# SSD chunks: the scaling by the reciprocal deviation is done by ScalarE instead of VectorE

## The chip, the cores and the metric

One core of a Trainium2 chip runs the whole program, a two-block sequence model on 1024 tokens of width 1024 in float32. The metric is the device time of one execution in microseconds (us). In three runs the kernel before took 3720.2, 3724.92 and 3739.85 us, median 3724.92.

Names of engines: PE is TensorE (PEld its weight loads), DVE is VectorE, ACT is ScalarE, POOL is GpSimd, SP is SyncE, which here only starts transfers.

## The reference, cut to what matters

The program computes a first block (short convolutions, a gated linear recurrence, a feed-forward part), then a second block with two mixers, the SSD mixer and an mLSTM, a projection and a routed mixture of experts. The change lies in the SSD mixer alone, in its last step, a norm over each of two groups of 512 channels:

```python
def group_rmsnorm(y, w, groups):
    b, l, c = y.shape
    yg = y.reshape(b, l, groups, c // groups)
    yg = yg * lax.rsqrt(jnp.mean(yg * yg, axis=-1, keepdims=True) + EPS)
    return yg.reshape(b, l, c) * w.astype(jnp.float32)

# inside ssd_mixer, for each chunk: y from inside the chunk, y from the carried state, the new state
cb = jnp.einsum('blgn,bsgn->bgls', c_c, b_c)
y = jnp.einsum('bgls,bgrls,bsgrp->blgrp', cb, lmat, x_c)
y = y + jnp.einsum('blgn,bgrpn,bgrl->blgrp', c_c, state, jnp.exp(a_cs))
...
y = y + d_skip.astype(f32)[:, None] * xs
y = y.reshape(bsz, seq, SSD_WIDTH) * jax.nn.silu(z.astype(f32))
return group_rmsnorm(y, norm_w, SSD_GROUPS).astype(z.dtype)
```

## The kernel before, in words

The function `ssd_chunks` (lines 1498 to 1862) runs the SSD mixer over NC = 8 chunks of 128 tokens. Tokens of a chunk lie on the 128 partitions, the 1024 channels along the free dimension: 16 heads of 64, in G = 2 groups of 8 heads. Each engine has its own written-out order of work, and semaphores tie the engines together. Chunk k's front part is done one chunk early, so each loop step k holds the rest of chunk k and the front of chunk k+1.

What each engine does in step k, in its order:

- **DVE** (lines 1724 to 1770): y of the carried state (L1728, reads PSUM), plus y inside the chunk (L1731, reads PSUM), plus the skip term (L1737), times silu(z) (L1739), the state's update (L1743, reads PSUM). Then for chunk k+1: `inputs` (L1686 xdt and L1689 xdec), `c_by_b` (L1693) and `matrices(k + 1, 0)` (L1699: the decay matrices of the first 8 heads times C by B, 128x1024). Then the reciprocal of chunk k's two deviations (L1751) and the scaling of y by them, two instructions of 128x512 (L1755). Then `matrices(k + 1, 1)` (L1699 again, the other 8 heads), the addition of the former chunk's output product to the residual (`add`, L1713, twice), the gain while the turned y is read from PSUM (L1767, twice), and the low half of the split into two parts for the float32 product (L1770). In step 0 `add` is replaced by the low halves of the second eight weight tiles (`w_low`, L1705).
- **ACT** (lines 1658 to 1676): copies of x and B out of PSUM for chunk k+1 (L1631, L1635), `decay(k + 1, 0)` (L1640, 8 exponentials of 128x128), the squares of y with their sums (L1665), the deviation (L1668, a square root), `decay(k + 1, 1)` (L1640, 8 more), in step 0 also the high halves of the second eight weight tiles (`w_high`, L1646), and at the end the high half of y (L1676). Square root and exponential use different tables, so each step has two table loads.
- **POOL** (lines 1612 to 1620): the state times its decay (L1616), the skip term of chunk k+1 (`skip`, L1605), the causal mask of chunk k+2 (`causal`, L1599: the broadcast cumulated decays plus the mask, 128x2048).
- **PE** (lines 1836 to 1862): y of the carried state (L1841), y inside the chunk (L1847, first and second group of heads each wait for their `matrices`), the new state (L1854), the turns of chunk k+1's x and B (L1794, L1799), C by B (L1806), the output product of chunk k-1 (`out_product`, 48 matmuls, L343 to L345), and last the turns of chunk k's normed y (`result`, L1827).
- **SP** (lines 1551 to 1575): the loads of chunk k+2, which wait for the state product of chunk k (xbc, then the broadcast of the cumulated decays L1559, then z), and at the start the 16 weight tiles of the output product through four buffers, each waiting for the `w_low` three tiles back (L1572).

PSUM's psA has two halves used in turn; `take` lets PE write a half only after its reader is through.

Of the kernel before, what the change touches and what calls it, by code (L numbers as in the profile page):

```python
# [16 lines left out]
ACT = mybir.ActivationFunctionType  # L17
ALU = mybir.AluOpType
# [6 lines left out]
def wait(eng, sem, value):  # L25

    if isinstance(value, int) and value <= 0:
        return
    eng.wait_ge(sem, value)  # L29
# [70 lines left out]
def f32(ap):  # L100
    return ap.bitcast(F32)
# [1396 lines left out]
def ssd_chunks(nc, A, x_tm, hl, scr):  # L1498
# [6 lines left out]
    NC, H, G, W = scr.T, SSD_HEADS, SSD_GROUPS, 1024  # L1505
    HG, HD, XT = H // G, W // H, W // P
    GW, HALF, NS = W // G, 512, 4
    with ExitStack() as ctx:
        c = Core(nc, ctx)
# [7 lines left out]
        x_r, xdt, xdec, xd = (c.sb(f"sd_{n}", [P, W]) for n in ("x", "xdt", "xdec", "xd"))  # L1517
        b_r, cbm = c.sb("sd_b", [P, G, P]), c.sb("sd_cb", [P, G, P])
        lt = c.sb("sd_l", [P, 2, H, P])
        state = c.sb("sd_state", [P, W])  # L1520
        y, sq = c.sb("sd_y", [P, W]), c.sb("sd_sq", [P, W])
        ssq, std, rstd = c.sb("sd_ssq", [P, G]), c.sb("sd_std", [P, G]), c.sb("sd_rstd", [P, G])
# [8 lines left out]
        s_w, s_whi, s_wlo = c.sems("w2_w_loaded", NS), c.sem("w2_w_high"), c.sem("w2_w_low")  # L1531
        (p_sums, p_A, p_cb, p_in, p_inter, p_state, p_w2) = (
            c.sem(f"sd_pe_{n}") for n in ("sums", "psA_written", "cb", "intra", "inter", "state", "out"))
        (a_e, a_A, a_l, a_sq, a_std, a_yh) = (c.sem(f"sd_act_{n}") for n in ("exps", "psA_read", "decay", "squares", "std", "high"))
        (d_xdt, d_xdec, d_cb, d_m, d_y1, d_yb, d_y, d_st, d_ch, d_rs, d_n, d_yt, d_yl, d_add) = (
            c.sem(f"sd_dve_{n}") for n in ("xdt", "xdec", "cb", "m", "y1", "psB_read", "y", "state", "chain", "rstd", "normed",
                                           "yt", "low", "added"))
        (g_x, g_l, g_st) = (c.sem(f"sd_pool_{n}") for n in ("x", "causal", "state"))
        block = ctx.enter_context(nc.Block(no_gpsimd_drain=True))
# [5 lines left out]
        def front_use(k, j):  # L1545
            return j if k == 0 else 5 * k - 2 + j

        def result_use(k, j):
            return 5 * k + (6 if k + 1 < NC else 3) + j
# [72 lines left out]
        @block.scalar  # L1622
        def _(act):
            def front(k):
                if k:
                    act.wait_ge(d_xdt, k)
                    act.wait_ge(g_x, k)
                for j in range(2):
                    n = front_use(k, j)
                    act.wait_ge(p_A, n + 1)  # L1630
                    nc.scalar.activation(x_r[:, j * 512:(j + 1) * 512], psA[:, n % 2], ACT.Copy).then_inc(a_A, 1)  # L1631
                n = front_use(k, 2)
                act.wait_ge(p_A, n + 1)
                wait(act, p_state, k)
                nc.scalar.activation(b_r[:].rearrange("p g n -> p (g n)"), psA[:, n % 2, 0:G * P], ACT.Copy).then_inc(a_A, 1)  # L1635

            def decay(k, g):
                act.wait_ge(g_l, k + 1)
                for h in range(g * HG, (g + 1) * HG):
                    last = nc.scalar.activation(lt[:, k % 2, h], lt[:, k % 2, h], ACT.Exp, bias=ncum[:, k, h:h + 1])  # L1640
                last.then_inc(a_l, 1)

            def w_high(n):
                h, k = divmod(n, XT)
                act.wait_ge(s_w[n % NS], 16 * (n // NS + 1))
                nc.scalar.activation(hl[:, 0, k, h * HALF:(h + 1) * HALF], stage[:, n % NS], ACT.Copy).then_inc(s_whi, 1)  # L1646

            act.wait_ge(s_c1, 6)
            act.wait_ge(p_sums, 1)
            nc.scalar.activation(ncum[:], sums[:, 0], ACT.Copy, scale=-1.0).then_inc(a_e, 1)  # L1650
            nc.scalar.activation(e3[:], sums, ACT.Exp).then_inc(a_e, 1)
            front(0)
            act.wait_ge(a_e, 2)
            decay(0, 0)
            decay(0, 1)
            for n in range(XT):
                w_high(n)
            for k in range(NC):
                if k + 1 < NC:
                    front(k + 1)  # L1660
                    decay(k + 1, 0)
                act.wait_ge(d_y, k + 1)
                for g in range(G):
                    cut = slice(g * GW, (g + 1) * GW)
                    nc.scalar.activation(sq[:, cut], y[:, cut], ACT.Square, accum_out=ssq[:, g:g + 1]).then_inc(a_sq, 1)  # L1665
                act.wait_ge(a_sq, G * (k + 1))
                wait(act, d_rs, k)
                nc.scalar.activation(std[:], ssq[:], ACT.Sqrt, scale=1.0 / GW, bias=eps[:]).then_inc(a_std, 1)  # L1668
                if k + 1 < NC:
                    decay(k + 1, 1)  # L1670
                if k == 0:
                    for n in range(XT, NW):
                        w_high(n)
                act.wait_ge(d_yt, 2 * k + 2)
                wait(act, p_w2, 2 * k)
                nc.scalar.activation(yh[:, 0], yt[:], ACT.Copy).then_inc(a_yh, 1)  # L1676

        @block.vector
        def _(dve):
            v, ch = nc.vector, Chain(dve, d_ch)  # L1680
# [10 lines left out]
            def c_by_b(k):  # L1691
                dve.wait_ge(p_cb, k + 1)
                v.tensor_copy(cbm[:], cbt).then_inc(d_cb, 1)  # L1693
                dve.wait_ge(d_cb, k + 1)
# [29 lines left out]
            for k in range(NC):  # L1724
                if k:
                    dve.wait_ge(p_inter, k)
                    dve.wait_ge(p_A, result_use(k - 1, 1) + 1)
                    v.tensor_tensor(heads(y[:]), both(psC), per_head(e3[:, 0, k]), ALU.mult).then_inc(d_y1, 1)  # L1728
                    dve.wait_ge(d_y1, k)
                    dve.wait_ge(p_in, k + 1)  # L1730
                    v.tensor_tensor(heads(y[:]), heads(y[:]), both(psB), ALU.add).then_inc(d_yb, 1)  # L1731
                else:
                    dve.wait_ge(p_in, 1)
                    v.tensor_copy(heads(y[:]), both(psB)).then_inc(d_yb, 1)
                dve.wait_ge(d_yb, k + 1)
                dve.wait_ge(g_x, k + 1)
                ch.link(v.tensor_tensor(y[:], y[:], xd[:], ALU.add))  # L1737
                dve.wait_ge(s_z[k % 2], 16 * (k // 2 + 1))
                v.tensor_tensor(y[:], y[:], z[:, k % 2], ALU.mult).then_inc(d_y, 1)  # L1739
                dve.wait_ge(p_state, k + 1)  # L1740
                if k:
                    dve.wait_ge(g_st, k)
                    v.tensor_tensor(state[:], state[:], psC[:].rearrange("p a n -> p (a n)"), ALU.add).then_inc(d_st, 1)  # L1743
                else:
                    v.tensor_copy(state[:], psC[:].rearrange("p a n -> p (a n)")).then_inc(d_st, 1)
                if k + 1 < NC:
                    inputs(k + 1)
                    c_by_b(k + 1)
                    matrices(k + 1, 0)
                dve.wait_ge(a_std, k + 1)  # L1750
                v.reciprocal(rstd[:], std[:]).then_inc(d_rs, 1)  # L1751
                dve.wait_ge(d_rs, k + 1)
                for g in range(G):
                    cut = slice(g * GW, (g + 1) * GW)
                    v.tensor_scalar(y[:, cut], y[:, cut], rstd[:, g:g + 1], None, ALU.mult).then_inc(d_n, 1)  # L1755
                if k + 1 < NC:
                    matrices(k + 1, 1)
                if k == 0:
                    for n in range(XT, NW):
                        w_low(n)  # L1760
                else:
                    add(k - 1)
                wait(dve, a_yh, k)
                for j in range(2):
                    n = result_use(k, j)
                    dve.wait_ge(p_A, n + 1)
                    v.tensor_tensor(yt[:, 4 * j:4 * j + 4], quad(n), norm[:, 4 * j:4 * j + 4].unsqueeze(2).to_broadcast([P, 4, P]),  # L1767
                                    ALU.mult).then_inc(d_yt, 1)
                dve.wait_ge(a_yh, k + 1)
                v.tensor_tensor(yh[:, 1], yt[:], f32(yh[:, 0]), ALU.subtract).then_inc(d_yl, 1)  # L1770
# [3 lines left out]
        def _(pe):  # L1774
# [8 lines left out]
            def take(n):  # L1783
                if n >= 2:
                    pe.wait_ge(*readers[n - 2])
# [33 lines left out]
                    last.then_inc(p_w2, 1)  # L1819

            def result(k):
                pe.wait_ge(d_n, G * (k + 1))
                for j in range(2):
                    n = result_use(k, j)
                    take(n)
                    for t in range(4):
                        last = nc.tensor.transpose(quad(n)[:, t], y[:, (4 * j + t) * P:(4 * j + t + 1) * P], ident[:])  # L1827
                    last.then_inc(p_A, 1)
# [1134 lines left out]
```

## Time and profile before

| what | value |
|---|---|
| three runs | 3720.2, 3724.92, 3739.85 us |
| the profiled execution, its own time | 3727.0 us |
| its span, first to last instruction | 3725.2 us |
| mean granted TensorE clock | 0.937 of full speed |
| the SSD chunks within the span | about 2407 to 2640 us |

The profile comes from one profiled execution. Its span is 1.8 us shorter than that execution's own time; what lies around the span is the launch and the end. In a row of the timeline the first number is the start in us from the span's start, the second the length in us, then engine, line, operation, output and inputs, shape, count (x2: two merged in one row). A bracket at the end gives the idle time of the engine before the row and the instruction that ended it. In a row of a line's summary three numbers stand for the shortest, the median and the longest in ns. In a row of stretches the columns are: the stretch in us, its length, busy time of PE, PEld, DVE, ACT and POOL with counts in brackets, the granted TensorE clock, the share of DMA and GB/s.

### The profile page before, as it was taken

What the parts mean: (1) busy time and instruction counts of PE and PEld (TensorE: products, weight loads), DVE (VectorE), ACT (ScalarE), POOL (GpSimd) and SP (SyncE); (2) the same over time, 40 slices, a digit from 0 to 9 for tenths busy, and PEclk for the clock granted to TensorE, in tenths of its full rate; (3) what the DMA queues carried; (4) which work ended last, traced back from release to release, by engine and by line L of the source; (5) the groups of instructions that cost most, each with busy time, mean ns of one, the idle gap of its engine ahead of it and who ended that gap; (6) DMA issues with size and microseconds to landing.
All of it is one profiled execution on the core that took longest, in us unless ns stands there. A gap on an engine that the chain in (4) does not pass through costs nothing. (4 is left out here: it accounts for less than half of the span.)

```text
span 3725.2 us, 39593 instructions
## 1 busy us (share of the span) xinstructions
PE 3361.8 (90%) x15130; PEld 2747.4 (74%) x15130; DVE 1930.8 (52%) x2158; ACT 1374.0 (37%) x1931; POOL 263.9 (7%) x312
## 2 busy tenths in 40 slices
PE   6999999898899999998799999869897859999994
PEld 4888888686788888887687788647787747777773
DVE  3344443433344455445413655188333468888885
ACT  4332332212321111111521323244255328788883
POOL 0000000000000000000010000133000110000002
PEclk9999999998999999999899999979766979999997
DMA  3222222433011111110331233642120239999996
GB/s 98 63 71 83 80 66 70 147 113 118 24 56 51 51 51 43 41 51 10 135 90 64 84 98 96 205 171 77 63 90 29 81 118 378 382 392 393 390 393 236
DMA packets 330352, 489.19 MB, mean 131 GB/s; under 512 B 58736, under 2 KB 230256, under 8 KB 328192
## 3 DMA queue, kind: packets, MB, share of 16 engines
q1 hardware_dynamic: 299776, 380.11, 29.8%
q0 software_dynamic: 25856, 90.78, 6.4%
q10 hardware_dynamic: 4608, 16.78, 1.1%
q8 instruction: 73, 1.20, 0.1%
q14 instruction: 39, 0.32, 0.0%
HBM read 406.28 MB, written 81.33 MB: 131 GB/s over the span
## 5 line engine op out<-in xcount | busy, mean ns | idle before, releaser
L947 DVE TENSOR_TENSOR x_rows<-x_rows,ff_psd 128x512 f32<-128x512 f32 x352 | 239.5, 688 | 334.5 <-PE ff_psd L345 334.5
L343 PE MATMUL m_ps<-h_hl,m_w_hl 128*128 128x512 f32 x896 | 356.7, 398 | 11.6 <-DVE m_w_hl L530 11.6
L345 PE MATMUL m_ps<-h_hl,m_w_hl 128*128 128x512 f32 x896 | 350.3, 391 | 0.0
L344 PE MATMUL m_ps<-h_hl,m_w_hl 128*128 128x512 f32 x896 | 350.2, 391 | 0.0
L2471 DVE TENSOR_TENSOR h_hl<-ex_stage,h_hl 128x1024 fp32r<-128x1024 f32 x256 | 306.1, 1222 | 45.2 <-ACT h_hl L2467 43.9
L2467 ACT ACTIVATE h_hl<-ex_stage 128x1024 fp32r<-128x1024 f32 x256 | 269.7, 1059 | 87.4 <-DMA ex_stage<-in_exp_w_up_dram 50.1
L343 PE MATMUL pj_turned<-h_hl,pc_w_hl 128*128 128x512 f32 x576 | 226.0, 392 | 6.1 <-DVE pc_w_hl L1310 6.1
L345 PE MATMUL pj_turned<-h_hl,pc_w_hl 128*128 128x512 f32 x576 | 225.0, 391 | 0.0
L344 PE MATMUL pj_turned<-h_hl,pc_w_hl 128*128 128x512 f32 x576 | 225.0, 391 | 0.0
L343 PEld LDWEIGHTS m_ps<-h_hl,m_w_hl 128*128 128x128 f32 x896 | 169.1, 189 | 50.5 <-DVE m_w_hl L530 12.0
L927 ACT ACTIVATE ff_act_hl<-ff_act 128x1024 fp32r<-128x1024 f32 x22 | 23.3, 1060 | 485.3 <-DVE ff_act L965 485.3
L344 PEld LDWEIGHTS m_ps<-h_hl,m_w_hl 128*128 128x128 f32 x896 | 169.0, 189 | 38.5 <-issue 3.8
L345 PEld LDWEIGHTS m_ps<-h_hl,m_w_hl 128*128 128x128 f32 x896 | 168.9, 188 | 35.2
L2471 DVE TENSOR_TENSOR ex_w_hl<-ex_stage,ex_w_hl 128x1024 fp32r<-128x1024 f32 x128 | 153.8, 1222 | 36.8 <-ACT ex_w_hl L2467 36.3
L530 DVE TENSOR_TENSOR m_w_hl<-m_stage,m_w_hl 128x1024 fp32r<-128x1024 f32 x56 | 68.5, 1223 | 193.9 <-ACT m_w_hl L458 193.9
L343 PE MATMUL ff_psg<-h_hl,ff_wg 128*128 128x512 f32 x352 | 139.9, 397 | 21.6 <-PE ff_psd L345 10.9
L2467 ACT ACTIVATE ex_w_hl<-ex_stage 128x1024 fp32r<-128x1024 f32 x128 | 132.8, 1057 | 45.5 <-DMA ex_stage<-in_exp_w_gate_dram 36.0
L343 PE MATMUL ff_psd<-ff_wd,ff_act_hl 128*128 128x512 f32 x352 | 138.2, 393 | 4.3 <-DVE ff_act_hl L967 4.3
L345 PE MATMUL ff_psg<-h_hl,ff_wg 128*128 128x512 f32 x352 | 138.0, 392 | 0.0
L344 PE MATMUL ff_psd<-ff_wd,ff_act_hl 128*128 128x512 f32 x352 | 138.0, 392 | 0.0
L344 PE MATMUL ff_psg<-h_hl,ff_wg 128*128 128x512 f32 x352 | 138.0, 392 | 0.0
L345 PE MATMUL ff_psd<-ff_wd,ff_act_hl 128*128 128x512 f32 x352 | 137.8, 391 | 0.0
(508 smaller groups left out, 7701.3 us busy)
## 6 DMA issues: line engine op xcount, KB each, us to landing
ex_stage<-in_exp_w_gate_dram SPq DMA_DIRECT2D x128, 512.0 KB, 5.5
ex_stage<-in_exp_w_up_dram SPq DMA_DIRECT2D x128, 512.0 KB, 7.6
ex_stage<-in_exp_w_down_dram SPq DMA_DIRECT2D x128, 512.0 KB, 6.3
m_stage<-in_w_in_dram SPq DMA_DIRECT2D x56, 512.0 KB, 4.2
pc_stage<-in_w_in_dram SPq DMA_DIRECT2D x36, 512.0 KB, 3.7
scratch_ys<-ex_ys ACTq DMA_DIRECT2D x32, 512.0 KB, 7.3
ff_stage<-in_w_ffn_gate_dram SPq DMA_DIRECT2D x22, 512.0 KB, 4.7
ff_stage<-in_w_ffn_up_dram SPq DMA_DIRECT2D x22, 512.0 KB, 6.0
```

The costliest lines, as they stand in the source:

```text
L343: nc.tensor.matmul(out, w_hl[0], x_hl[0], start=first, stop=False)
L344: nc.tensor.matmul(out, w_hl[0], x_hl[1], start=False, stop=False)
L345: return nc.tensor.matmul(out, w_hl[1], x_hl[0], start=False, stop=last)
L530: v.tensor_tensor(w_hl[s][:, 1], stage[:, s], f32(w_hl[s][:, 0]), ALU.subtract).then_inc(s_lo, 1)
L927: nc.scalar.activation(a_hl[b][:, 0], act_f[:], ACT.Copy).then_inc(s_ah, 1)
L947: v.tensor_tensor(dst, dst, ps_d[g % NB][:], ALU.add).then_inc(s_add, 1)
L2467: nc.scalar.activation(w_hl[u][:, 0], stage[:, s], ACT.Copy).then_inc(s_hi, 1)
L2471: nc.vector.tensor_tensor(w_hl[u][:, 1], stage[:, slot(e, u)], f32(w_hl[u][:, 0]), ALU.subtract).then_inc(s_lo, 1)
```

## The change

The two scalings leave the DVE's order, where they stood behind the reciprocal, and enter ACT's order behind the square root and ahead of `decay(k + 1, 1)`. ACT now waits for the reciprocal before them. DVE's reciprocal waits for the former chunk's scalings, since they read what it overwrites. PE's turns of y wait for ACT instead of DVE.

```diff
@@ ACT, step k
                 act.wait_ge(a_sq, G * (k + 1))
                 wait(act, d_rs, k)
                 nc.scalar.activation(std[:], ssq[:], ACT.Sqrt, scale=1.0 / GW, bias=eps[:]).then_inc(a_std, 1)
+                act.wait_ge(d_rs, k + 1)
+                for g in range(G):
+                    cut = slice(g * GW, (g + 1) * GW)
+                    nc.scalar.activation(y[:, cut], y[:, cut], ACT.Copy, scale=rstd[:, g:g + 1]).then_inc(a_n, 1)
                 if k + 1 < NC:
                     decay(k + 1, 1)
@@ DVE, step k
                 dve.wait_ge(a_std, k + 1)
+                wait(dve, a_n, G * k)
                 v.reciprocal(rstd[:], std[:]).then_inc(d_rs, 1)
-                dve.wait_ge(d_rs, k + 1)
-                for g in range(G):
-                    cut = slice(g * GW, (g + 1) * GW)
-                    v.tensor_scalar(y[:, cut], y[:, cut], rstd[:, g:g + 1], None, ALU.mult).then_inc(d_n, 1)
                 if k + 1 < NC:
                     matrices(k + 1, 1)
@@ PE, result(k)
-                pe.wait_ge(d_n, G * (k + 1))
+                pe.wait_ge(a_n, G * (k + 1))
```

## Rows read from the trace of the kernel before

**Rows 1.** The page, part 1: busy time of each engine over the span

```profile
PE 3361.8 (90%) x15130; PEld 2747.4 (74%) x15130; DVE 1930.8 (52%) x2158; ACT 1374.0 (37%) x1931; POOL 263.9 (7%) x312
```

**Rows 2.** Stretches: chunk 2 and chunk 5 of the SSD stage

```profile
2496.80:2518.90 22.10, 21.03 (x112) 16.48 (x112) 20.77 (x20) 11.41 (x27) 9.26 (x3) 1.00 0.27 108
...
2563.10:2587.00 23.90, 22.83 (x113) 17.12 (x112) 22.15 (x20) 11.41 (x27) 9.79 (x3) 0.93 0.26 100
```

**Rows 3.** Summary of line 1755, all chunks

```profile
L1755 DVE TENSOR_SCALAR sd_y<-sd_y,sd_rstd x16: 473/484/4667, 2456.6 to 2619.4; 128x512 f32<-128x512 f32 x16
```

**Rows 4.** Timeline of DVE in chunk 2

```profile
2506.53 1.23 DVE L1699 TENSOR_TENSOR sd_l<-sd_l,sd_cb 128x1024 f32<-128x1024 f32 x1
...
2507.67 0.16 DVE L1751 RECIPROCAL sd_rstd<-sd_std 128x2 f32<-128x2 f32 x1
...
2507.87 5.06 DVE L1755 TENSOR_SCALAR sd_y<-sd_y,sd_rstd 128x512 f32<-128x512 f32 x2
...
2512.85 1.21 DVE L1699 TENSOR_TENSOR sd_l<-sd_l,sd_cb 128x1024 f32<-128x1024 f32 x1
...
2517.58 1.39 DVE L1770 TENSOR_TENSOR sd_y_hl<-sd_yt,sd_y_hl 128x1024 fp32r<-128x1024 f32 x1 [1.12 <-ACT sd_y_hl L1676]
```

**Rows 5.** Timeline of POOL in chunk 2

```profile
2506.79 5.46 POOL L1599 TENSOR_TENSOR sd_l<-sd_cum_l,sd_neg 128x2048 f32<-128x2048 f32 x1 [2.97 <-DMA sd_cum_l<-scratch_cum]
...
2515.99 1.90 POOL L1616 TENSOR_TENSOR sd_state<-sd_state,sd_e 128x1024 f32<-128x1024 f32 x1 [3.74 <-PE sd_psC L1841]
```

**Rows 6.** Timeline of ACT in chunk 2

```profile
2506.98 0.29 ACT L1668 ACTIVATE sd_std<-sd_ssq,sd_eps 128x2 f32<-128x2 f32 x1
...
2507.30 1.28 ACT L1640 ACT_TABLE_LOAD   x1
...
2508.59 2.45 ACT L1640 ACTIVATE sd_l<-sd_l,sd_neg_cum 128x128 f32<-128x128 f32 x8
```

**Rows 7.** Summaries of ACT lines: exponentials, copies, a copy with a scale per partition

```profile
L1640 ACT ACTIVATE sd_l<-sd_l,sd_neg_cum x128: 384/388/404, 2419.3 to 2602.5; 128x128 f32<-128x128 f32 x128
...
L1646 ACT ACTIVATE h_hl<-w_stage x16: 615/631/635, 2434.6 to 2466.4; 128x512 fp32r<-128x512 f32 x16
...
L1676 ACT ACTIVATE sd_y_hl<-sd_yt x8: 1056/1057/1057, 2469.0 to 2628.9; 128x1024 fp32r<-128x1024 f32 x8
...
L232 ACT ACTIVATE n_xn<-x_rows,n_rstd x32: 1131/1146/1154, 10.8 to 2998.9; 128x1024 f32<-128x1024 f32 x32
```

**Rows 8.** Timeline of DVE in chunk 0

```profile
2456.38 0.16 DVE L1751 RECIPROCAL sd_rstd<-sd_std 128x2 f32<-128x2 f32 x1
...
2457.37 1.22 DVE L1699 TENSOR_TENSOR sd_l<-sd_l,sd_cb 128x1024 f32<-128x1024 f32 x1
```

**Rows 9.** Timeline of DVE in chunk 1

```profile
2484.35 5.58 DVE L1699 TENSOR_TENSOR sd_l<-sd_l,sd_cb 128x1024 f32<-128x1024 f32 x1
...
2489.86 0.15 DVE L1751 RECIPROCAL sd_rstd<-sd_std 128x2 f32<-128x2 f32 x1
...
2490.85 1.22 DVE L1699 TENSOR_TENSOR sd_l<-sd_l,sd_cb 128x1024 f32<-128x1024 f32 x1
```

**Rows 10.** Timeline of POOL in chunk 1

```profile
2484.23 4.63 POOL L1599 TENSOR_TENSOR sd_l<-sd_cum_l,sd_neg 128x2048 f32<-128x2048 f32 x1 [2.58 <-DMA sd_cum_l<-scratch_cum]
...
2493.88 1.90 POOL L1616 TENSOR_TENSOR sd_state<-sd_state,sd_e 128x1024 f32<-128x1024 f32 x1 [5.03 <-PE sd_psC L1841]
```

**Rows 11.** Timeline of PE: the state product of chunks 1 and 2

```profile
2472.48 2.93 PE L1854 MATMUL sd_psC<-sd_xdec,sd_b 128*128 128x512 f32 x3 [6.42 <-DVE sd_y L1728]
...
2498.05 1.98 PE L1854 MATMUL sd_psC<-sd_xdec,sd_b 128*128 128x512 f32 x4 [0.73 <-DVE sd_y L1728]
```

**Rows 12.** Timeline of DVE in chunk 6

```profile
2599.16 0.17 DVE L1751 RECIPROCAL sd_rstd<-sd_std 128x2 f32<-128x2 f32 x1
...
2602.93 1.23 DVE L1699 TENSOR_TENSOR sd_l<-sd_l,sd_cb 128x1024 f32<-128x1024 f32 x1 [2.68 <-ACT sd_l L1640]
...
2608.23 2.61 DVE L1770 TENSOR_TENSOR sd_y_hl<-sd_yt,sd_y_hl 128x1024 fp32r<-128x1024 f32 x1 [1.12 <-ACT sd_y_hl L1676]
```

More of the change, by code:

```diff
@@ L1533, in ssd_chunks @@
             c.sem(f"sd_pe_{n}") for n in ("sums", "psA_written", "cb", "intra", "inter", "state", "out"))
-        (a_e, a_A, a_l, a_sq, a_std, a_yh) = (c.sem(f"sd_act_{n}") for n in ("exps", "psA_read", "decay", "squares", "std", "high"))
-        (d_xdt, d_xdec, d_cb, d_m, d_y1, d_yb, d_y, d_st, d_ch, d_rs, d_n, d_yt, d_yl, d_add) = (
-            c.sem(f"sd_dve_{n}") for n in ("xdt", "xdec", "cb", "m", "y1", "psB_read", "y", "state", "chain", "rstd", "normed",
+        (a_e, a_A, a_l, a_sq, a_std, a_yh, a_n) = (c.sem(f"sd_act_{n}") for n in ("exps", "psA_read", "decay", "squares", "std", "high", "normed"))
+        (d_xdt, d_xdec, d_cb, d_m, d_y1, d_yb, d_y, d_st, d_ch, d_rs, d_yt, d_yl, d_add) = (
+            c.sem(f"sd_dve_{n}") for n in ("xdt", "xdec", "cb", "m", "y1", "psB_read", "y", "state", "chain", "rstd",
                                            "yt", "low", "added"))
```

## The prediction

> **What bounds the kernel now.** The page's busy shares [rows 1] are means over the whole program and say little: the change touches only the SSD stage, 233 us of the span. I read the stretches of that stage chunk by chunk: DVE is busy 20.77 of 22.10 us in chunk 2, PE 21.03 of 22.10 at full granted clock [rows 2]. Chunks 3 and 4 look the same. So DVE and PE are both nearly full here, while ACT works half the time.
>
> The summary of line 1755 shows what the change is aimed at: a scaling takes 0.48 us in the median but 4.67 us at worst [rows 3]. The timelines show the cause. In chunk 2 the pair starts at 2507.87 while POOL's mask sum runs from 2506.79 to 2512.25, and takes 5.06 us instead of 0.88 [rows 4, 5]. Chunks 2 to 5, four of eight, have it; the other four pairs take 0.88. In chunk 1 the same mask sum starts 0.12 us ahead of `matrices(2, 0)`, and that instruction is the one stretched, to 5.58 us against 1.22 [rows 9, 10]. So it is not the scaling that is special: the DVE instruction that comes while POOL's runs is held to its end. In the rows the L1699 of 1.21 us, the L1770 and the scaling all behave so, the reciprocal of two columns does not [rows 4].
>
> What decides the change stands beside this on ACT. After the deviation (ends 2507.27) come the table load, 1.28 us, and eight exponentials, 2.45 us, which end at 2511.04 [rows 6]. DVE's next instruction, the second L1699, needs them. DVE asks for them only at 2512.85 [rows 4]: DVE's stall covers the exponentials.
>
> **The change part by part.** The yardstick is the stretch from the end of the reciprocal to the start of the second L1699.
>
> Removed from DVE: the pair, 5.06 us in four chunks and 0.88 in four [rows 3, 4].
>
> Added to ACT, behind the reciprocal: two copies of 128x512 with a scale per partition. The plain copy of that size takes 0.63 us. A scale per partition costs the copy of 1024 columns 1.146 - 1.057 = 0.09 us [rows 7]. So 0.72 each; neighbours overlap, since eight exponentials of 0.388 (sum 3.10) take 2.45, or 0.09 at each of seven joints [rows 6, 7]. Two come to 2 x 0.72 - 0.09 = 1.35 us. Bounds: 1.17 without the scale's extra, 1.44 without overlap.
>
> Moved on ACT: table load and exponentials now stand behind that. The new stretch from the reciprocal's end is 0.03 (a semaphore, as from 2507.27 to 2507.30 [rows 6]) + 1.35 + 0.03 + 1.28 + 0.01 + 2.45 + 0.03 = 5.18 us. Bounds 5.0 and 5.3. No table load is added: between square root and exponential one is there already, and line 1676's copies follow either function without one.
>
> The Trainium skill (ScalarE: Activation LUTs, What ACT_TABLE_LOAD costs) adds about 1.38 us of drain to a switch of tables. Here the exponentials start 0.01 us after the load, so the trace does not agree; with the page's figure the stretch would be 6.6 us and the whole sum some 8 us higher.
>
> Chunks 2 to 5: the reciprocal ends at 2507.83 in chunk 2, so L1699 starts at 2513.0 instead of 2512.85: +0.16 us [rows 4]. The mask sum is over by then, so it isn't stretched. Even 0.16 is hidden: L1770 is held to 1.39 us by POOL's state scaling (ends 2517.89), which PE's order releases, not DVE's [rows 4, 5]. It ends at 2518.97 either way. Four times zero: **the 4.2 us stall that goes is replaced by a wait for ACT of the same length.**
>
> Chunk 0: no stall was there. The reciprocal ends at 2456.54; L1699 moves from 2457.37 [rows 8] to 2461.72, **+4.35 us**. Behind it are the low halves of eight weight tiles, and SP's last four weight loads and chunk 2's loads wait for these, so SP's queue moves along and nothing absorbs it. On ACT the high halves queue behind the exponentials and shift by as much.
>
> Chunk 1: the reciprocal ends at 2490.01, after L1699's stall. The second L1699 moves from 2490.85 to 2495.19. PE's turns, after the last scaling, come at 2491.4 instead of 2490.99, and with them POOL's state scaling goes from 2493.88 to about 2494.3, ending 2496.2 [rows 9, 10]. L1699 now falls into it and is held until 1.08 us after its end (as L1770 in chunk 2): ends 2497.3 instead of 2492.07, **+5.2 us**.
>
> Chunk 2, PE: its state product waits for DVE's L1728. That idle time was 0.73 us and is then 4 to 5 us. In chunk 1, after 6.42 us of idling, three matmuls took 0.98 us apiece against 0.50 [rows 11]: the lower of the two clock levels. What this costs a chunk is the difference of chunk 5 (granted 0.93) and chunk 2 (1.00): 23.9 - 22.1 = **1.8 us** [rows 2]. Bounds 0 and 1.8; I take it whole, since the idle time is nearer to the 6.42 than to the 0.73.
>
> Chunk 6: the pair took 0.88 and DVE waited 2.68 us for ACT already; L1699 moves from 2602.93 to 2599.33 + 5.18 = 2604.5, +1.6, of which the adds' wait for PE takes some. The rest goes into L1770's stretch, 2.61 against 1.22, a slack of 1.39 [rows 12]: zero, bound 0.5. Chunk 7 has no second L1699, and its turns on PE wait for the output product beyond both dates: zero. POOL's queue issues no transfer in these chunks.
>
> Sum: 4.35 + 5.2 + 1.8 = 11.35 us. The profiled execution took 3727.0 us, so 3738.4 against its own time. It lies 2.1 us above the median of 3724.92, so against the median 3736.
>
> **The rivals.** *The freed stall counts (faster).* If the exponentials were not late, DVE would win 4 x 5.06 + 4 x 0.88 = 23.8 us: 3701. For it: DVE is 94% busy. Against it: the 5.18 us of ACT's new chain, and POOL's hold on L1770, which would eat the gain even then. Half of it would be 3713. Chance 0.04.
>
> *Chunk 1 slips out (a little slower).* The mask sum starts only 0.12 us ahead of L1699 there [rows 9, 10]. If it starts behind, L1699 runs through in 1.2, the reciprocal comes 4.4 us earlier, and chunk 1 costs nothing, as chunk 2 does. Left is chunk 0: +4.4, 3729. Chance 0.2.
>
> *The stall lands ahead of the reciprocal in more chunks (slower).* In chunk 2 the first L1699 starts 0.26 us before the mask sum, whose transfer decides when [rows 4, 5]. Before, the order didn't matter: the chunk lost one stall either way. After the change the order matters: a stretched L1699 delays the reciprocal, and the 5.18 us come on top. Each chunk that turns pays what chunk 1 pays, 5.2 us. One gives 3741; all four of chunks 2 to 5 give 11.35 + 20.8 = 32, 3757. It is slower by over 0.5% (18.6 us) from the second chunk on. Chance of exactly one 0.2, of more 0.09.
>
> The Trainium skill (SBUF — State Buffer, SBUF: two separate sides) has the mechanism as an exclusive lock on a port pair that DVE and GpSimd share, taken by whoever starts first, by DVE for two SBUF inputs as well as for its two-port modes. By that rule L1699, with two SBUF inputs, inherits any wait that the scaling gives up, and the trace agrees: 5.58 us in chunk 1.
>
> **How the numbers follow.** Forecast (sum of 7 to 16 us) 0.47, with the time 3736. Slipped chunk 0.2, one chunk more 0.2, more 0.09, faster 0.04. From 3725 (the slipped chunk with a low median) to 3748 (one chunk more, with the runs' own spread and the high bounds) lie over 8 in 10; this leaves out the faster rival and the several turned chunks. About 0.5% is what a measurement of this kernel can tell from no change, 18.6 us. The forecast, the slipped chunk and one chunk more lie inside: same 0.88, slower 0.09, faster 0.03.
>
> **What would show it.** Right: the second L1699 of chunks 0 to 6 starts 5.2 us after the reciprocal's end, each time with an idle time that ACT's exponentials end; two copies of y on ACT, 1.35 us together; no table load more than before; chunks 2 to 5 as long as before; chunks 0 and 1 longer by 4 to 5 us; a slow state product in chunk 2. Wrong: a DVE that reaches the next chunk earlier in chunks 2 to 5, a stretched first L1699 in more chunks than chunk 1, or a difference outside the SSD stage.

## The result, and the profile after

The changed kernel takes 3733.78 us in the median of 20 runs (3720.2 to 3750.2), the kernel before 3726.06 (20 runs, 3718.86 to 3739.85). The ratio is 1.0024, interval 1.0013 to 1.0036: slower by a quarter of a per cent, some 9 us. A second measurement (the first experiment) gave 1.0033, 1.0016 to 1.0051. The forecast had been 11 us, with the time 3736, range 3725 to 3748.

The profiled execution of the changed kernel took 3748.45 us, among the slowest of its 20; its span is 3746.7 us, 21.5 more than before. Two stretches, first of the kernel before and then of the changed one, show how much of that is in the SSD stage (columns: the stretch and its length, busy time of PE, PEld, DVE, ACT and POOL with counts, granted clock, DMA share, GB/s):

```profile
2407.70:2644.50 236.80, 186.16 (x882) 142.34 (x882) 174.68 (x159) 101.87 (x234) 74.92 (x34) 0.86 0.32 116
```

```profile
2406.90:2661.00 254.10, 190.52 (x882) 144.95 (x882) 156.58 (x143) 112.83 (x250) 75.69 (x34) 0.83 0.30 108
```

The stage is 17.3 us longer; the other 4 us lie behind it, in the expert stage above all. From line 232's last instruction to the end that stage took 721 to 733 us in the twelve profiles, whose kernels share it, so nothing of this is put down to the change; that none of it belongs to the change isn't shown. ACT's count goes up by 16 and DVE's down by 16, the sixteen scalings. No table load was added: line 1640 has seven and line 1668 eight, as before.

Now the answers to [rows 4, 8, 9]. DVE in chunk 0, chunk 1, chunk 2 and chunk 5. Line 1703 is the old 1699 and 1756 the old 1751:

```profile
2455.72 0.16 DVE L1756 RECIPROCAL sd_rstd<-sd_std 128x2 f32<-128x2 f32 x1
...
2461.05 1.23 DVE L1703 TENSOR_TENSOR sd_l<-sd_l,sd_cb 128x1024 f32<-128x1024 f32 x1 [5.17 <-ACT sd_l L1640]
...
2488.12 5.43 DVE L1703 TENSOR_TENSOR sd_l<-sd_l,sd_cb 128x1024 f32<-128x1024 f32 x1
...
2493.47 0.15 DVE L1756 RECIPROCAL sd_rstd<-sd_std 128x2 f32<-128x2 f32 x1
...
2498.79 2.13 DVE L1703 TENSOR_TENSOR sd_l<-sd_l,sd_cb 128x1024 f32<-128x1024 f32 x1 [5.17 <-ACT sd_l L1640]
...
2517.45 5.70 DVE L1703 TENSOR_TENSOR sd_l<-sd_l,sd_cb 128x1024 f32<-128x1024 f32 x1
...
2523.07 0.15 DVE L1756 RECIPROCAL sd_rstd<-sd_std 128x2 f32<-128x2 f32 x1
...
2528.40 2.13 DVE L1703 TENSOR_TENSOR sd_l<-sd_l,sd_cb 128x1024 f32<-128x1024 f32 x1 [5.17 <-ACT sd_l L1640]
...
2592.79 1.23 DVE L1703 TENSOR_TENSOR sd_l<-sd_l,sd_cb 128x1024 f32<-128x1024 f32 x1
...
2593.93 0.16 DVE L1756 RECIPROCAL sd_rstd<-sd_std 128x2 f32<-128x2 f32 x1
...
2599.28 1.23 DVE L1703 TENSOR_TENSOR sd_l<-sd_l,sd_cb 128x1024 f32<-128x1024 f32 x1 [5.19 <-ACT sd_l L1640]
```

What to see: between the reciprocal and the second L1703 DVE now does nothing at all, and each time the bracket names the exponentials (L1640). From the reciprocal's end to that start it is 5.17 us in chunk 0 and 5.19 in chunk 5. In chunk 5 the whole distance from the first L1703 to the second is 6.49 us, against 6.32 in [rows 4]: the pair's 5.06 us have gone and a wait of the same size stands there. ACT shows what fills it, in chunk 5 and for the first line in chunk 1:

```profile
2493.66 1.33 ACT L1672 ACTIVATE sd_y<-sd_y,sd_rstd 128x512 f32<-128x512 f32 x2 [5.82 <-DVE sd_rstd L1756]
...
2594.12 1.34 ACT L1672 ACTIVATE sd_y<-sd_y,sd_rstd 128x512 f32<-128x512 f32 x2 [0.57 <-DVE sd_rstd L1756]
...
2595.49 1.28 ACT L1640 ACT_TABLE_LOAD   x1
...
2596.78 2.46 ACT L1640 ACTIVATE sd_l<-sd_l,sd_neg_cum 128x128 f32<-128x128 f32 x8
```

Two copies 1.34 us, table load 1.28, exponentials 2.46. POOL, in chunks 1, 2 and 5, as in [rows 5, 10]:

```profile
2487.86 4.61 POOL L1599 TENSOR_TENSOR sd_l<-sd_cum_l,sd_neg 128x2048 f32<-128x2048 f32 x1 [2.44 <-DMA sd_cum_l<-scratch_cum]
...
2497.94 1.90 POOL L1616 TENSOR_TENSOR sd_state<-sd_state,sd_e 128x1024 f32<-128x1024 f32 x1 [5.48 <-PE sd_psC L1842]
...
2517.44 4.62 POOL L1599 TENSOR_TENSOR sd_l<-sd_cum_l,sd_neg 128x2048 f32<-128x2048 f32 x1 [1.44 <-DMA sd_cum_l<-scratch_cum]
...
2593.12 5.38 POOL L1599 TENSOR_TENSOR sd_l<-sd_cum_l,sd_neg 128x2048 f32<-128x2048 f32 x1 [3.03 <-DMA sd_cum_l<-scratch_cum]
```

In chunk 1 the mask sum starts 0.26 us ahead of the first L1703, which is held for 5.43 us. The same happens in chunk 2, where POOL is first by 0.01 us; in the kernel before DVE was first by 0.26 us there. In chunk 5 DVE is first by 0.33 us and runs through in 1.23. In chunks 1 and 2 the second L1703 takes 2.13 us, because it falls into POOL's state scaling (2497.94 to 2499.84 in chunk 1).

PE's state product, in chunks 2 and 4, as in [rows 11]:

```profile
2506.86 3.78 PE L1855 MATMUL sd_psC<-sd_xdec,sd_b 128*128 128x512 f32 x4 [3.31 <-DVE sd_y L1732]
...
2560.22 3.68 PE L1855 MATMUL sd_psC<-sd_xdec,sd_b 128*128 128x512 f32 x4 [0.74 <-DVE sd_y L1732]
```

Both took about 3.7 us for four matmuls, against 1.98 in [rows 11]. The difference is the clock: in the kernel before the profile grants 1.00 of full speed (2.4 GHz) over the short product of chunk 4 and 0.54, nearly all of it the lower level of 1.2 GHz, over the long one of chunk 5. In the rows above the first came after 3.31 us of idling, the second after 0.74. Chunks 1, 2, 3, 4 and 7 have a long one, chunks 5 and 6 don't; before they were chunks 1, 5, 6 and 7.

From one L1728 (now L1732) to the next, chunk lengths before were 25.6, 22.1, 22.1, 22.1, 23.8 and 23.8 us for chunks 1 to 6. After, in this execution, they are 30.6, 29.6, 23.8, 24.1, 22.1 and 22.1. Chunk 0 grew by 4.6.

### The profile page after: what moved, and what is told of

Its sections match the earlier page's. It is cut to its first block and busy times, and to the rows that moved or that the text cites. A ratio compares the mean times of both kernels' runs of the same rounds, so it can differ in the third digit from the quotient of the medians.

```text
span 3746.7 us, 39600 instructions
## 1 busy us (share of the span) xinstructions
PE 3365.5 (90%) x15130; PEld 2746.7 (73%) x15130; DVE 1912.0 (51%) x2142; ACT 1386.0 (37%) x1947; POOL 266.1 (7%) x312
## 3 DMA queue, kind: packets, MB, share of 16 engines
q1 hardware_dynamic: 299776, 380.11, 29.7%
## 5 line engine op out<-in xcount | busy, mean ns | idle before, releaser
L927 ACT ACTIVATE ff_act_hl<-ff_act 128x1024 fp32r<-128x1024 f32 x22 | 23.4, 1062 | 485.3 <-DVE ff_act L965 485.3
```

The costliest lines, as they stand in the source:

```text
L927: nc.scalar.activation(a_hl[b][:, 0], act_f[:], ACT.Copy).then_inc(s_ah, 1)
```

## The experiments

The ratio compares each kernel with the kernel before, timed beside it: 20 executions of the changed kernel in the first measurement, 11 or 12 in most others, 8 in e8 and only 4 in e7. All columns behind the ratio come from one profiled execution each. The stage is measured from the first instruction of the SSD chunks to the first of the mLSTM behind them, chunk 0 from the same first instruction to the first L1728. "Long products" counts the state products of chunks 1 to 7 that take over 2.5 us (the expectations call them slow). All in us.

| kernel | ratio and interval | stage | chunk 0 | chunk 1 | chunk 2 | long products |
|---|---|---|---|---|---|---|
| before | | 237.6 | 63.5 | 25.6 | 22.1 | 4 |
| changed | 1.0024, 1.0013 to 1.0036 | 254.9 | 68.1 | 30.6 | 29.6 | 5 |
| e1 changed, again | 1.0033, 1.0016 to 1.0051 | 242.3 | 67.2 | 29.7 | 23.7 | 2 |
| e2 swap | 1.0005, 0.9992 to 1.0018 | 235.8 | 65.3 | 26.7 | 22.1 | 1 |
| e3 swap in chunk 0 | 1.0039, 1.0024 to 1.0054 | 251.3 | 67.0 | 30.5 | 23.8 | 7 |
| e8 the same, again | 1.0041, 1.0021 to 1.0062 | 251.4 | 66.6 | 30.9 | 23.8 | 7 |
| e9 swap in chunks 0, 1 | 1.0008, 0.9995 to 1.0020 | 239.1 | 65.8 | 26.1 | 22.1 | 3 |
| e4 changed, mask late | 1.0024, 1.0011 to 1.0037 | 241.5 | 67.5 | 25.7 | 23.4 | 4 |
| e10 swap in 0, mask late | 1.0014, 1.0002 to 1.0026 | 238.1 | 66.7 | 25.5 | 24.3 | 2 |
| e5 before, mask late | 1.0017, 1.0008 to 1.0026 | 238.9 | 66.4 | 25.8 | 24.5 | 2 |
| e6 before, forced order | 0.9997, 0.9987 to 1.0006 | 241.3 | 66.2 | 25.8 | 22.6 | 3 |
| e7 changed, forced order | 1.0108, 1.0093 to 1.0124 | 273.5 | 68.3 | 30.9 | 29.5 | 6 |

**The changed kernel again (e1).** No edit.

> The changed kernel itself, once more. My theory (the two scalings put 5.2 us in front of the second eight exponentials, and DVE waits for these): the second L1703 of chunks 0 to 6 starts 5.2 us after the reciprocal's end in every chunk; chunk 0 costs about 4.4 us and chunk 1 about 5 against before; chunk 2 costs 5 to 7 only if its first L1703 is stretched by POOL's mask sum, and that happens in some executions and not in others. Expected time 6 to 12 us over the kernel before, ratio 1.002 to 1.003. Rival (the state product at the lower clock after DVE's lateness is part of the price): one more slow state product in every profile than in the profile of before, which has three.

Median 3735.71 against 3723.29 us, +12.4, a little over what was expected. The profiled execution took 3723.64, nearly the fastest of the twelve: its stage is 4.7 us longer than in the profile of before, but what follows the stage is 6.6 us shorter. So this profile and the one above stand for the two ends of the changed kernel's spread, and none for its middle. The idle time in front of the second L1703 is again 5.2 us in every chunk, and chunk 1 again has its stretched first L1703. In this execution chunk 2 kept its order: DVE 0.39 us ahead of POOL (first two rows), the L1703 short, and the chunk 23.7 us long.

```profile
2514.08 1.23 DVE L1703 TENSOR_TENSOR sd_l<-sd_l,sd_cb 128x1024 f32<-128x1024 f32 x1
...
2514.47 5.31 POOL L1599 TENSOR_TENSOR sd_l<-sd_cum_l,sd_neg 128x2048 f32<-128x2048 f32 x1 [1.84 <-DMA sd_cum_l<-scratch_cum]
...
2528.11 1.98 PE L1855 MATMUL sd_psC<-sd_xdec,sd_b 128*128 128x512 f32 x4 [0.73 <-DVE sd_y L1732]
```

So chunk 2 turning (its first L1703 coming second and being held) is a matter of the execution, as expected. The rival, one long product more in every profile than in that of before, is wrong: before has four (the expectation says three), this profile two, and from chunk 3 on all state products are like the third row, 1.98 us.

**Exponentials first, then the scalings (e2).**

```diff
@@
                 nc.scalar.activation(std[:], ssq[:], ACT.Sqrt, scale=1.0 / GW, bias=eps[:]).then_inc(a_std, 1)
+                if k + 1 < NC:
+                    decay(k + 1, 1)
                 act.wait_ge(d_rs, k + 1)
@@
                     nc.scalar.activation(y[:, cut], y[:, cut], ACT.Copy, scale=rstd[:, g:g + 1]).then_inc(a_n, 1)
-                if k + 1 < NC:
-                    decay(k + 1, 1)
                 if k == 0:
```

> ACT runs the second eight exponentials first and the two scalings behind them. My theory: the loss is the place in ACT's order, not the engine. DVE's second L1703 no longer waits for the scalings; the turns of y get them 1.35 us after the reciprocal or after the exponentials, which PE's output product covers from chunk 2 on. Time equal to the kernel before within 2 us (ratio 0.9990 to 1.0007), 8 to 10 us below the changed kernel. In chunks 2 to 5 the second L1703 starts at once when the exponentials end and is stretched by what is left of the mask sum, about 1 to 2 us. Rival (the loss is the scaling on ACT itself, slower by 0.5 us a pair and one engine crossing): 4 to 8 us over the kernel before still. Rival (the freed stall counts once the wait is gone): 10 us or more under the kernel before.

Ratio 1.0005, 8 us under the changed kernel of the same measurement: most of the loss is gone, though the scalings are still on ACT. So the order on ACT was the cause and not the engine, as far as the interval goes: its upper end, 1.0018, still leaves room for the smaller part of the first rival's 4 to 8 us. The gain of 10 us or more that the second rival promised is excluded. DVE in chunk 2:

```profile
2509.64 1.23 DVE L1703 TENSOR_TENSOR sd_l<-sd_l,sd_cb 128x1024 f32<-128x1024 f32 x1
...
2510.78 0.16 DVE L1756 RECIPROCAL sd_rstd<-sd_std 128x2 f32<-128x2 f32 x1
...
2514.19 2.24 DVE L1703 TENSOR_TENSOR sd_l<-sd_l,sd_cb 128x1024 f32<-128x1024 f32 x1 [3.25 <-ACT sd_l L1640]
```

DVE waits 3.3 us for the exponentials, and the second L1703 then takes 2.24 us instead of 1.23, held by the rest of the mask sum. The chunk is 22.12 us, as in the kernel before: what the scaling doesn't wait for, the next instruction does.

**The swap in chunk 0 alone (e3), and once more (e8).**

```diff
@@
                 nc.scalar.activation(std[:], ssq[:], ACT.Sqrt, scale=1.0 / GW, bias=eps[:]).then_inc(a_std, 1)
+                if k == 0:
+                    decay(k + 1, 1)
                 act.wait_ge(d_rs, k + 1)
@@
                     nc.scalar.activation(y[:, cut], y[:, cut], ACT.Copy, scale=rstd[:, g:g + 1]).then_inc(a_n, 1)
-                if k + 1 < NC:
+                if k and k + 1 < NC:
                     decay(k + 1, 1)
```

> The swap in chunk 0 alone; chunks 1 to 7 as in the changed kernel. My theory: chunk 0's 4.4 us go (its second L1703 starts right behind the reciprocal), the rest stays: 4 to 5 us below the changed kernel, 2 to 6 above the kernel before. Rival (chunk 0's delay is absorbed by the weight loads): no difference to the changed kernel.

It came out at 1.0039, 3742.14 us in the median: 6 us above the changed kernel's median, not 4 to 5 below (the intervals overlap, so that it is slower isn't shown). This expectation failed.

> The swap in chunk 0 alone, once more, since it came out slower than the changed kernel instead of 4 us faster. Its one profile showed all seven state products behind chunk 0 at the lower clock, against one in the profile of the changed kernel of the same call; that is up to 1.7 us a chunk. If that belongs to this kernel: again 3740 us or more, and again six or seven slow state products. If it was that execution's luck: about 3733 us, and two to four slow ones. If my chunk 0 term was right besides: the second instruction of L1705 in chunk 0 starts 3 us or less after the reciprocal instead of 5.2.

1.0041 again, so the missing gain belongs to the kernel and not to one measurement. DVE in chunk 0 of e3, and PE's state products of chunks 2, 3 and 4:

```profile
2457.58 1.23 DVE L1705 TENSOR_TENSOR sd_l<-sd_l,sd_cb 128x1024 f32<-128x1024 f32 x1 [3.06 <-ACT sd_l L1640]
...
2504.32 3.67 PE L1857 MATMUL sd_psC<-sd_xdec,sd_b 128*128 128x512 f32 x4 [3.88 <-DVE sd_y L1734]
...
2528.12 3.68 PE L1857 MATMUL sd_psC<-sd_xdec,sd_b 128*128 128x512 f32 x4 [0.74 <-DVE sd_y L1734]
...
2551.94 3.65 PE L1857 MATMUL sd_psC<-sd_xdec,sd_b 128*128 128x512 f32 x4 [0.73 <-DVE sd_y L1734]
```

Two things are seen. In chunk 0 DVE still waits 3.06 us for the exponentials, where in [rows 8] it could start the second L1699 0.83 us after the reciprocal's end: the front of ACT's work was itself late in this execution, since its copies of x waited 3.0 us for PE's turns, against 0.1 us in the profile of before. e8 has the same 3.07 us, and e5 and e6, which are the kernel before in this place, 2.9 and 3.2. Of the twelve profiles, only those of before, of the changed kernel and of e4 have ACT early in chunk 0; in the others the change can cost 2 us there and not 4.35. Why ACT is early in some executions isn't known. Second, all seven state products are long, in both runs, those of chunks 3 to 7 after only 0.74 us of idling, and chunks 2 to 6 are 23.8 to 24.1 us long. The row begins behind a chunk 1 of over 30 us with PE idle for 3.88 us. That is what the last two experiments took up.

**The mask sum only after the reciprocal (e4).**

```diff
@@
                 if k + 2 < NC:
+                    pool.wait_ge(d_rs, k + 1)
                     causal(k + 2)
```

> The changed kernel, and POOL starts the mask sum of chunk k+2 only after chunk k's reciprocal, so the first L1703 is never stretched. My theory: the race ahead of the reciprocal is what chunks 1 and 2 pay; with it gone the mask sum runs entirely within the 5.2 us in which DVE waits for ACT. Chunks 1 and 2 then take what they took before (chunk 1 about 25.5 us, chunk 2 about 22 to 24), only chunk 0's 4.4 us stay: ratio 1.001 to 1.0015, and the spread of the runs is smaller than the changed kernel's. Rival (chunk 1 pays for the exponentials whatever POOL does): chunk 1 stays at 30 us.

DVE and POOL in chunk 1:

```profile
2489.61 1.22 DVE L1704 TENSOR_TENSOR sd_l<-sd_l,sd_cb 128x1024 f32<-128x1024 f32 x1
...
2490.76 0.16 DVE L1757 RECIPROCAL sd_rstd<-sd_std 128x2 f32<-128x2 f32 x1
...
2496.08 1.23 DVE L1704 TENSOR_TENSOR sd_l<-sd_l,sd_cb 128x1024 f32<-128x1024 f32 x1 [5.17 <-ACT sd_l L1641]
...
2490.99 4.59 POOL L1599 TENSOR_TENSOR sd_l<-sd_cum_l,sd_neg 128x2048 f32<-128x2048 f32 x1 [4.09 <-DVE sd_rstd L1757]
```

The first L1703 runs through in 1.22 us, the mask sum (2490.99 to 2495.58) fits into ACT's 5.2 us, and chunk 1 takes 25.70 us instead of 30. So the rival falls: chunk 1 pays for the stretched instruction ahead of the reciprocal and not for the exponentials alone. The spread is smaller too, 3724.96 to 3738.75 against 3723.32 to 3750.11. The ratio is 1.0024 where I expected 1.001 to 1.0015. Part of it is chunk 2: PE still idles 2.9 us and its product is long. The intervals of e1 and e4 overlap, so the time saved can't be told from the medians; that chunk 1 got shorter rests on the profile.

**The same in the kernel before (e5).** Is the stall worth anything where it stood?

```diff
@@
                 if k + 2 < NC:
+                    pool.wait_ge(d_n, G * (k + 1))
                     causal(k + 2)
```

> The kernel before, with POOL's mask sum of chunk k+2 only after chunk k's two scalings, so that these never wait for it. My theory: the stall isn't worth anything. The pairs take 0.88 us in all eight chunks, 17 to 20 us of DVE time go, but the second L1699 then waits for the exponentials (about 2 us) and is itself held by the mask sum; chunk lengths stay 22.1 us or 23.8 with a slow state product; ratio 0.999 to 1.001. Rival (the stall was a real loss, and the change only failed to collect it): 3705 to 3712 us, ratio 0.995 to 0.997.

Summary of the scaling's line over all chunks, and DVE's second L1699 (here 1700) in chunk 2:

```profile
L1756 DVE TENSOR_SCALAR sd_y<-sd_y,sd_rstd x16: 479/485/491, 2452.5 to 2617.8; 128x512 f32<-128x512 f32 x16
...
2511.98 3.24 DVE L1700 TENSOR_TENSOR sd_l<-sd_l,sd_cb 128x1024 f32<-128x1024 f32 x1 [2.55 <-ACT sd_l L1641]
```

The longest scaling takes 491 ns, against 4667 in [rows 3]: the stall is gone completely. The kernel is a little slower, 1.0017. The second L1699 takes 3.24 us after waiting 2.55 for ACT. My expectation of 0.999 to 1.001 was a little off, to the slow side, and why isn't known; the rival's gain of 13 to 20 us is excluded.

**DVE made to come second, in the kernel before (e6) and in the changed one (e7).** From step 1 on the front waits for the transfer that releases the mask sum:

```diff
@@
                     inputs(k + 1)
+                    if k and k + 2 < NC:
+                        dve.wait_ge(s_cum, 16 * (k + 3))
                     c_by_b(k + 1)
```

> The kernel before, with DVE's copy of C by B (and so the first L1699) of chunks 2 to 6, in steps 1 to 5, only after the cumulated decays that the mask sum waits for have landed, so that POOL always starts first and the first L1699 is the one stretched. My theory: the kernel before doesn't mind which of its instructions waits, since the pair behind is then short: 0 to 1 us a chunk, 0 to 4 us in all, ratio 1.000 to 1.001. Rival (every stretched first L1699 costs its 4.4 us in any order of work): 15 to 20 us, ratio 1.004 to 1.005.

> The same forced order in the changed kernel. My theory: each of chunks 2 to 5 now pays for both, the stretched first L1703 and behind it the 5.2 us of scalings, table load and exponentials, as chunk 1 does: chunk lengths of 28 to 30 us, 20 to 30 us over the changed kernel, ratio 1.008 to 1.011 to the kernel before. Rival (ACT's waiting hides behind PE's output product): under 8 us over the changed kernel, ratio below 1.005.

DVE in chunk 2, first of e6 and then of e7:

```profile
2509.77 5.29 DVE L1699 TENSOR_TENSOR sd_l<-sd_l,sd_cb 128x1024 f32<-128x1024 f32 x1
...
2514.98 0.15 DVE L1753 RECIPROCAL sd_rstd<-sd_std 128x2 f32<-128x2 f32 x1
...
2515.96 1.22 DVE L1699 TENSOR_TENSOR sd_l<-sd_l,sd_cb 128x1024 f32<-128x1024 f32 x1
```

```profile
2522.07 5.29 DVE L1703 TENSOR_TENSOR sd_l<-sd_l,sd_cb 128x1024 f32<-128x1024 f32 x1
...
2527.29 0.15 DVE L1758 RECIPROCAL sd_rstd<-sd_std 128x2 f32<-128x2 f32 x1
...
2532.61 2.13 DVE L1703 TENSOR_TENSOR sd_l<-sd_l,sd_cb 128x1024 f32<-128x1024 f32 x1 [5.17 <-ACT sd_l L1640]
```

In both the first instruction takes 5.29 us. In e6 the second follows 0.98 us after the reciprocal's start; in e7 5.32 us, and it is stretched to 2.13 besides. e6 costs nothing that can be told, 0.9997. e7 takes 3768.7 us in the median of its four executions (3760.45 to 3770.3) against 3725.4, +43, with chunks 1 to 5 between 29.1 and 30.9 us. This is the plainest result of the study: the kernel before doesn't mind which of its instructions waits for POOL, the changed one does.

**The swap in chunks 0 and 1 (e9), and in chunk 0 with the mask late (e10).** e9 replaces `k == 0` by `k < 2` in e3's edit, e10 adds e4's wait to e3.

```diff
@@ e9, against e3
-                if k == 0:
+                if k < 2:
                     decay(k + 1, 1)
...
-                if k and k + 1 < NC:
+                if k >= 2 and k + 1 < NC:
                     decay(k + 1, 1)
@@ e10, against e3
                 if k + 2 < NC:
+                    pool.wait_ge(d_rs, k + 1)
                     causal(k + 2)
```

> The swap in chunks 0 and 1, where my sum puts the loss; chunks 2 to 7 as in the changed kernel, scalings ahead of the exponentials. My theory: chunks 2 to 5 cost nothing there unless the first L1703 is stretched, so the time is that of the full swap: ratio 1.000 to 1.0015, 7 us or more under the swap in chunk 0 alone. Chunk 1 takes 26 to 27 us instead of 30.5, chunks 2 to 6 take 22.1 or 23.8 by the state product's clock. Rival (the loss is spread over all chunks): 1.003 or more.

> The swap in chunk 0 alone, with the mask sum only after the reciprocal. Both runs of the swap in chunk 0 alone had PE idle for 3.9 us in chunk 2 ahead of the state product, behind a chunk 1 with two stretched L1703, and then seven slow state products in a row. Theory A (the long chunk 1 sets off the row of slow products): chunk 1 is 25.7 us here, PE idles 3 us at most, the row breaks up into three slow products or fewer, ratio 1.001 to 1.002. Theory B (the row belongs to the place in time to which the swap moves the chunks, not to chunk 1's length): five or more slow ones here too, ratio 1.003 or more.

e9: 1.0008, chunk 1 26.1 us, chunks 2 to 4 22.1 to 22.4 with the scalings ahead of the exponentials. So the loss sits in chunks 0 and 1 and what they set off; the order of chunks 2 to 5 costs nothing unless one of them turns. e10: 1.0014, chunk 1 25.5 us, two long products, as theory A has it; theory B, five or more, fails. With the swap in chunk 0 the row came in both profiles with a long chunk 1 and not in the one with a short chunk 1. But a long chunk 1 alone doesn't set it off: e1 has one of 29.7 us and no row. PE's products of chunks 2 and 3 in e10:

```profile
2501.25 3.78 PE L1858 MATMUL sd_psC<-sd_xdec,sd_b 128*128 128x512 f32 x4 [2.32 <-DVE sd_y L1735]
...
2525.59 1.98 PE L1858 MATMUL sd_psC<-sd_xdec,sd_b 128*128 128x512 f32 x4 [0.73 <-DVE sd_y L1735]
```

Why a row goes on with chunks of 23.8 us in e3 and e8 and breaks off in e1, e4 and the changed kernel's profile is not settled.

## Why the prediction was right, and where it was off

- **The stall is replaced, not removed.** Right. The stretch behind the reciprocal was to be 5.18 us; it is 5.16 to 5.19 in every chunk that has the scalings in front, in all profiles. Its terms: copies 1.34 (1.35), table load 1.28, exponentials 2.46 (2.45). The drain of 1.38 us that the Trainium skill (ScalarE: Activation LUTs, What ACT_TABLE_LOAD costs) adds behind a table load isn't there: the exponentials start 0.01 us after it.
- **Chunks 2 to 5 cost zero.** Right where DVE comes first and the product is short: 22.1 to 22.4 us in chunks 3 to 5 of e1 and 2 to 4 of e9. The gain that the freed stall would bring is excluded by e2 and e5.
- **Chunk 0, 4.35 us.** Right against the profile of before (4.6), but too large as a term of the kernels' difference. The step that failed read the second eight exponentials' readiness off one chunk 0. In the seven other profiles with the old order or the swap in chunk 0 they came 3 us after the reciprocal, which leaves 2 us: chunk 0 took 66.2 and 66.4 us in e6 and e5, 67.2 to 68.3 in the changed order.
- **Chunk 1, 5.2 us.** Right in kind and size: +5.0 in the profile after and +4.1 in e1. Both of its parts were seen, the stretched first instruction ahead of the reciprocal (e4 takes it away and chunk 1 returns to 25.7) and the second one in POOL's state scaling (2.13 us). In e1 the second part is missing: DVE came first, and its L1703 took 1.23 us.
- **Chunk 2, the long state product, 1.8 us.** It is there in all profiles of the changed kernel, with e4's and e7's among them, behind 2.9 to 3.3 us of idling, where the forecast had 4 to 5. But long products also come after 0.74 us of idling, in chunks 5 to 7 of the kernel before as well, which the prediction passed over: it took the clock elsewhere as fixed. It isn't: the number of long ones went from one to seven between kernels of the same work, and from e1 to e3 that is 8.5 of the stage's us (chunks 2 to 6 together 6.8, chunk 7 to the end 1.7).
- **More chunks turning.** That was the slower rival, from one chunk on at 5.2 us each. Chunk 2 turned in the profiled execution and cost 7.5 us with its long product; by the prediction's own signs of being wrong, this execution shows one, and the e1 profile doesn't. The price of 5.2 us was too low: in e7, with four chunks turned besides chunk 1, the stage is 36 us longer than in the profile of before where the sum said 32, since PE's state products are long in every such chunk (chunks 2 to 4 grew by 7.0 to 7.9 us each). Its time is 43 us longer; the other 7 us aren't explained.
- **The sum.** With the sizes found, about 2 for chunk 0, 4 to 5 for chunk 1 and 1.7 for chunk 2, it is 8 to 9 us for an execution in which no other chunk turns; the first measurement gave 9, the second 12. That the forecast of 11 came so near is in part luck: two errors worked against each other, a chunk 0 term too large and occasional turning left out of the sum.
- **What can be told.** The prediction took 0.5% as the least difference that a measurement of this kernel shows. The intervals are about 0.12% to either side with twenty executions, so a loss of 0.24% can be told from no change.

The rule of the Trainium skill (SBUF — State Buffer, SBUF: two separate sides) was the right guide: the wait belongs to the port pair and not to the instruction. By its rule an instruction with two SBUF inputs inherits the wait that the scaling gives up, and the traces agree: 2.24 us in e2, 3.24 in e5, 5.4 and 5.7 in the changed kernel. It is spared only where DVE has nothing to do while the mask sum runs, as in e4.

No version beats the kernel before; the full swap (e2) can't be told from it and leaves the scalings on ACT.

## What to carry to other kernels

Before work is moved off an engine because it stalls there, look what the next instruction on that engine needs, and when that comes: here the stall covered eight exponentials, and the work was moved in front of just these. Where two engines contend for a port, ask which orders of arrival the kernel tolerates: a stall that covers another wait costs nothing, a stall ahead of a newly added round trip between engines is paid on top of it. In a queue that another engine waits for, put the moved work behind what is waited for.

## What the runs showed of the hardware that was not expected

- A DVE instruction of two SBUF inputs that starts 0.01 us after POOL's (2517.45 against 2517.44) is held for 5.70 us; one that starts 0.26 us ahead is not, and POOL's instruction is then the longer one (5.46 us in [rows 5] against 4.62). Each held L1703 ended about 1.1 us after POOL's instruction.
- The state product's four matmuls take 1.98 or some 3.7 us after the same 0.74 us of idling. In e3 and e8 the long case repeated through chunks 3 to 7, at 23.8 to 24.1 us for each of chunks 3 to 6; in e1 the short one did, at 22.1 to 22.4.
